# One ones-matmul per head instead of several: VectorE adds key tiles elementwise before TensorE sums over partitions

## What is computed

```python
s = jnp.einsum('bhtd,bhsd->bhts', qb, kb) * jnp.exp(dlog - m_t[..., None])
num = jnp.einsum('bhts,bhsd->bhtd', s, vb) + inter[..., None] * jnp.einsum('bhvk,bhtk->bhtv', C, qb)
den = jnp.sum(s, axis=-1) + inter * jnp.einsum('bhk,bhtk->bht', n, qb)
h = num / jnp.maximum(jnp.abs(den), jnp.exp(-m_t))[..., None]
n_new = decay[..., None] * n + jnp.einsum('bht,bhtk->bhk', wk, kb)
...
hm = hm * lax.rsqrt(jnp.mean(hm * hm, axis=-1, keepdims=True) + EPS)
```

## Time and profile before

| what | value |
|---|---|
| time, median of 3 runs | 1107.98 us (1105.71 to 1108.42) |
| the profiled execution's own time | 1107.28 us |
| its span in the trace | 1105.5 us |
| TensorE busy | 980.7 us, 89% |
| VectorE busy | 675.6 us, 61% |
| ScalarE busy | 551.7 us, 50% |
| GpSimd busy | 286.7 us, 26% |
| mean granted TensorE clock | 0.947 of full |

### The profile page before, as it was taken

How to read it: one execution, slowest core, us unless ns; L and a number is a source line. 1 busy time by engine, 2 the same in 40 slices (tenths; PEclk the granted TensorE clock), 3 DMA queues, 4 the chain that set the end, 5 groups by cost and what they waited for, 6 DMA issues and landing times.

```text
span 1105.5 us, 16710 instructions
## 1 busy us (share of the span) xinstructions
PE 980.7 (89%) x5991; PEld 864.3 (78%) x5991; DVE 675.6 (61%) x820; ACT 551.7 (50%) x610; POOL 286.7 (26%) x192
## 2 busy tenths in 40 slices
PE   3989899999999969799999999837699999999950
PEld 2989789889978958699999976736588888888740
DVE  5495569658848863512111113377889898989738
ACT  5644524715544451423333214434777888887624
POOL 3443213403412240633434433010011110101024
PEclk9989999999999989899999999958899999999985
DMA  9342221313212200123233277135999999999734
GB/s 310 115 158 59 63 67 46 93 38 85 71 48 67 76 19 20 58 77 95 79 92 92 79 197 276 68 128 206 380 397 411 412 414 410 413 413 410 283 113 169
DMA packets 146737, 193.66 MB, mean 175 GB/s; under 512 B 14486, under 2 KB 91692, under 8 KB 146576
## 3 DMA queue, kind: packets, MB, share of 16 engines
q1 hardware_dynamic: 139000, 165.27, 43.4%
q0 software_dynamic: 4656, 16.21, 3.8%
q10 hardware_dynamic: 3048, 11.75, 2.7%
HBM read 173.43 MB, written 19.77 MB: 175 GB/s over the span
## 4 chain that ended last, share of the span: by engine, by line
PE 72%; DVE 14%; issue 5%; DMA 4%; ACT 4%; POOL 0%; DVEq 0%; SPq 0%; ACTq 0%; POOLq 0%
PE PJ L447 58%; DVE MEM L1629 2%; DVE MEM_R L1835 2%; PE MS L1285 2%; PE NM L1265 2%; PE PJ L1214 1%; PE MS L1247 1%; PE MS L1448 1%; DMA CHUNK<-in_w_up_dram 1%; DMA RAW<-in_w_out_dram 1%; PE MS L1292 1%; PE MS L1260 1%; DMA MEM<-t_rows,MEM 1%; PE NM L1479 1%; PE NM L1396 1%
## 5 line engine op out<-in xcount | busy, mean ns | idle before, releaser
L447 PE MATMUL PJ<-MEM_R 128*128 128x272 f32 (+2 forms) x5016 | 812.8, 323 | 22.3 <-DVE MEM_R L1945 6.8
L447 PEld LDWEIGHTS PJ<-MEM_R 128*128 128x128 f32 x5016 | 730.5, 193 | 86.3 <-issue 10.3
L660 POOL TENSOR_TENSOR MEM_R<-RAW,MEM_R 128x1024 fp32r<-128x1024 f32 x81 | 201.5, 2495 | 374.9 <-ACT MEM_R L796 374.7
L1835 DVE TENSOR_TENSOR MEM_R<-CHUNK,MEM_R 128x2048 fp32r<-128x2048 f32 x100 | 224.9, 2287 | 29.1 <-ACT MEM_R L1054 28.9
L1054 ACT CAST MEM_R<-CHUNK 128x2048 fp32r<-128x2048 f32 x100 | 189.5, 1914 | 30.7 <-DMA CHUNK<-in_w_gate_dram 16.0
L796 ACT CAST MEM_R<-RAW 128x1024 fp32r<-128x1024 f32 x81 | 84.6, 1053 | 133.7 <-DMA RAW<-in_w_pb_dram 39.3
L1775 DVE TENSOR_TENSOR MERGED<-PJ,MEM 128x544 f32<-128x544 f32 x16 | 11.6, 724 | 148.4 <-PE PJ L447 148.4
L742 POOL COPY MEM<-MEM 128x1 uint32 (+1 forms) x18 | 17.0, 946 | 268.3 <-PE MS L1448 242.9
L1629 DVE SCALAR_TENSOR_TENSOR MEM<-MEM 128x548 f32<-128x548 f32 x72 | 60.9, 845 | 8.5 <-DVE MEM L1629 0.5
L1063 ACT CAST MEM_R<-MS 128x1024 fp32r<-128x1024 f32 x17 | 17.3, 1016 | 35.3 <-PE MS L1448 35.3
L1247 PE MATMUL MS<-MEM 128*128 128x512 f32 (+4 forms) x80 | 23.3, 437 | 11.7 <-DVE MEM L1669 11.6
(11 more groups left out here) (285 smaller groups left out, 942.5 us busy)
## 6 DMA issues: line engine op xcount, KB each, us to landing
CHUNK<-in_w_gate_dram SPq DMA_DIRECT2D x34, 1024.0 KB, 6.8
CHUNK<-in_w_up_dram SPq DMA_DIRECT2D x34, 1024.0 KB, 8.5
CHUNK<-in_w_down_dram SPq DMA_DIRECT2D x34, 1024.0 KB, 7.0
RAW<-in_w_in_dram SPq DMA_DIRECT2D x56, 512.0 KB, 3.7
expert_rows<-MEM ACTq DMA_DIRECT2D x16, 512.0 KB, 6.0
expert_rows<-MEM SPq DMA_DIRECT2D x8, 512.0 KB, 5.2
RAW<-in_w_pa_dram SPq DMA_DIRECT2D x8, 512.0 KB, 3.7
RAW<-in_w_pb_dram SPq DMA_DIRECT2D x8, 512.0 KB, 3.6
```

What stands on the lines that cost most here:

```text
L447: ins = pe.matmul(out, w(a), x(b), start=first and n == 0, stop=last and n == 2)
L660: tt(lo, raw[slot], hi.bitcast(F32), ALU.subtract).then_inc(lo_done, 1)
L1835: tt(moe_hl[c][1], moe_raw[c], moe_hl[c][0].bitcast(F32), ALU.subtract).then_inc(chunk_lo[c], 1)
```

## The change

In `probabilities`, after the weighted keys, VectorE adds the four key tiles' `dp` for queries 128 to 511 into a new tile `dsum` (three adds of 384, 256 and 128 columns; it lies in the place of `sq`), and the four prompt tiles of `kw` into `ksum` (one add of 512 columns, one of 256; it lies in `rs[:, 1]`). A new step `squares_sum` adds the two channel tiles of `sq` in place (544 columns); it stands between `distances(hd)` and `new_state(hd-1)`, in the last head between `head_results` and `new_state`. TensorE's use 9 is then two matmuls, the first tile's queries 0 to 127 (128 columns) and `dsum` (384 columns), in place of four of 512, 384, 256 and 128; use 13 has one 256-column matmul for the prompt in place of four; uses 14 and 15 have one matmul each in place of two. Three semaphores carry the new waits.

```diff
@@ -195,6 +195,7 @@
         ri = tmp[:, 0:2, :], at("kw", 2, LN_)
         hh = at("tmp", CT, N)
         sq = at("tmp", CT, N, plus=CT * N)
+        dsum = at("tmp", LP - P, plus=CT * N)
         dp = at("dp", J, 512)
         v, kw = at("v", J, HD), at("kw", J, HD)
         c0, c0t = at("c0", CT, HD), at("c0t", CT, HD)
@@ -202,6 +203,7 @@
         nout = at("nout", 2, HD)
         og = at("og", CT, N)
         rs = at("rs", 2, N)
+        ksum = at("rs", 2, HD, plus=N)
         qs = at("qs", CT, LS)
         n0rep = at("n0rep", CT, P)
         n0row = at("n0row", HD)[0:1]
@@ -362,6 +364,7 @@
         conv_done, sig_ready, silu_done = sem("conv_done"), sem("sig_ready"), sem("silu_done")
         decay_ready, poly_ready, root_ready, lru_done = sem("decay_ready"), sem("poly_ready"), sem("root_ready"), sem("lru_done")
         sq_ready, rms_root, my_done = sem("sq_ready"), sem("rms_root"), sem("my_done")
+        dsum_ready, ksum_ready, sq_summed = sem("dsum_ready"), sem("ksum_ready"), sem("sq_summed")
         branch_hi, last_states, rows_copied = sem("branch_hi"), sem("last_states"), sem("rows_copied")
         branch_split = [sem(f"branch_split{m}") for m in range(2)]
         mix_full, sig_done, mul_done, merged_split = sem("mix_full"), sem("sig_done"), sem("mul_done"), sem("merged_split")
@@ -391,7 +394,7 @@
         NCONST, NLATE = 12, 13
         ORDER = [JP] + list(range(JP))
         HALF = D // 2
-        V_HEAD = 61
+        V_HEAD = 64
         FIN_P = 3
         NCT2 = D // P
         NPJ, NMS = PJ_LOOP + (H - 1) * PJ_HEAD, MS_PRE + H * MS_HEAD
@@ -1256,9 +1259,9 @@
             def numerators(hd):
 
                 b = ms_use(9, hd)
-                for j in range(JP):
-                    last = pe.matmul(b[:, P * j:LP], ones, dp[:, j, P * j:LP], start=j == 0, stop=j == JP - 1)
-                filled(last)
+                pe.wait_ge(dsum_ready, hd + 1)
+                pe.matmul(b[:, 0:P], ones, dp[:, 0, 0:P], start=True, stop=True)
+                filled(pe.matmul(b[:, P:LP], ones, dsum, start=True, stop=True))
                 pe.wait_ge(nm_free, hd + 1)
                 for c in range(CT):
                     for j in range(JP):
@@ -1286,19 +1289,15 @@
                                              start=j == tiles[0], stop=j == tiles[-1])
                     filled(last)
                 b = ms_use(13, hd)
-                for m, tiles in enumerate((range(JP), [JP])):
-                    for j in tiles:
-                        n = rows_of[j]
-                        last = pe.matmul(b[:, m * HD:(m + 1) * HD], ones[0:n, :], kw[0:n, j, :], start=j == tiles[0], stop=j == tiles[-1])
-                filled(last)
+                pe.wait_ge(ksum_ready, hd + 1)
+                pe.matmul(b[:, 0:HD], ones, ksum[:, 0, :], start=True, stop=True)
+                filled(pe.matmul(b[:, HD:2 * HD], ones[0:LS, :], kw[0:LS, JP, :], start=True, stop=True))
 
             def head_squares(hd):
-                pe.wait_ge(sq_ready, hd + 1)
+                pe.wait_ge(sq_summed, hd + 1)
                 for u, toks in ((14, slice(0, LP)), (15, slice(LP, N))):
                     b = ms_use(u, hd)
-                    for c in range(CT):
-                        last = pe.matmul(b[:, 0:toks.stop - toks.start], ones, sq[:, c, toks], start=c == 0, stop=c == CT - 1)
-                    filled(last)
+                    filled(pe.matmul(b[:, 0:toks.stop - toks.start], ones, sq[:, 0, toks], start=True, stop=True))
 
             for g in range(4):
                 project(0, g)
@@ -1678,6 +1677,17 @@
                     ins = ts(kw[0:n, j, :], b[0:n, (j % 2) * HD:(j % 2) * HD + HD], gcol[0:n, j, ds(hd + H, 1)], None, ALU.mult)
                     emptied(ins) if j % 2 or j == JP else st.do(ins)
 
+                st.link(tt(dsum, dp[:, 0, P:LP], dp[:, 1, P:LP], ALU.add))
+                st.link(tt(dsum[:, P:], dsum[:, P:], dp[:, 2, 2 * P:LP], ALU.add))
+                tt(dsum[:, 2 * P:], dsum[:, 2 * P:], dp[:, 3, 3 * P:LP], ALU.add).then_inc(dsum_ready, 1)
+                dve.wait_ge(ms_free, hd * MS_HEAD + (MS_PRE + 2 + 9))
+                st.link(tt(ksum, kw[:, 0:2, :], kw[:, 2:4, :], ALU.add))
+                tt(ksum[:, 0, :], ksum[:, 0, :], ksum[:, 1, :], ALU.add).then_inc(ksum_ready, 1)
+
+            def squares_sum(hd):
+                dve.wait_ge(sq_ready, hd + 1)
+                tt(sq[:, 0, :], sq[:, 0, :], sq[:, 1, :], ALU.add).then_inc(sq_summed, 1)
+
             def head_results(hd):
 
                 den, b = misc(hd, 9), misc(hd, 10)
@@ -1741,6 +1751,7 @@
                 head_results(hd - 1)
                 silu(hd, 0)
                 distances(hd)
+                squares_sum(hd - 1)
                 new_state(hd - 1)
                 conv(hd, 1)
                 conv(hd, 2)
@@ -1753,6 +1764,7 @@
                 second_part(hd)
             probabilities(H - 1)
             head_results(H - 1)
+            squares_sum(H - 1)
             new_state(H - 1)
             mean_squares(H - 1)
             branch_rows(H - 1)
```

## The result

| | before | after |
|---|---|---|
| median of its runs | 1107.03 us (1105.71 to 1108.42, 4 runs) | 1094.63 us (1094.31 to 1095.30, 4 runs) |
| profiled execution: span, mean granted clock | 1105.5 us, 0.947 | 1092.1 us, 0.949 |

The ratio of the times, after over before, is 0.9892 with a 95% interval of 0.9875 to 0.9910: the changed kernel is faster by 12.0 us (10 to 13.8). Two further batches of it gave 0.9906 and 0.9875. One later run of the kernel before fell into a slow state (1443 us, at a mean granted clock of 0.649) and is in no ratio and no mean.

What follows compares the result with a forecast made beforehand. TensorE was taken to bound the heads until the weighted-key sums (L1292), then VectorE's chain up to the values. Gains of 2.6, 2.8, 2.6 and 1.3 us summed to 9.3 us, giving 1098.7 us; range 1095.5 to 1106.

Steps and rivals of the forecast that it cites:

- Step 1: Denominator, use 9 on TensorE: 2.16 us become 0.86, 1.30 us saved a head, on the path in all four.
- Step 2: `dsum` and `ksum` adds on VectorE: 3 us a head, swallowed by its 10.41 us wait before L1686; cost 0.
- Step 3: New normaliser, use 13, before L1708: 2.56 us become about 1.0, 1.5 us saved in each of three passes.
- Step 4: Squares, uses 14 and 15: 2.08 us halved to 1.04, but the values' wait grows to some 1.5; gain 0.
- Step 5: `squares_sum` before L1705: 0.73 us add passes GpSimd's L660; L1292 about 0.2 us later in passes one and three, hidden in two.
- Step 6: Last head: L1720's pair waits for GpSimd's L694, which moves by step 1 alone; gain 1.3 us, 3.8 if neither is caught.
- GpSimd gets in first: Rival, chance 0.34: GpSimd's L660 blocks `squares_sum`, delaying L1705 and L1292; gain only 3.9 us, 1104.1 us.
- Everything counts: Rival, chance 0.05: all TensorE savings, squares included, count, 3.84 us in each of four heads, 15.3 us; 1092.7 us.
- The clock falls: Rival, chance 0.07: TensorE idles longer at the values or before L1292, adding 1.2 GHz stretches of 1.4 us each; 1112.5 us.

Runs made afterwards that it cites:

- its own experiment: The kernel before with only the `ksum` part, that is use 13's prompt matmuls and its two adds: ratio 0.9943, 6.3 us faster.
- the old kernel's third trace: The kernel before, unchanged, traced again to compare stages: span 1104.4 us.
- the kernel with the add 0.16 us behind: The changed kernel with a tiny memset and a wait for its end in front of the squares' add: 1101.45 us, ratio 0.9941.

## Why the prediction was right, and by how much it missed

- **Step 1**, right: 0.87 us are left of 2.16, the pass is 1.3 us shorter by it.
- **Step 2**, right: cost 0, with 2.9 us in hand before L1263 and 6.93 us of wait left on VectorE.
- **Step 3**, right in place, 0.2 us too large: the four records take 1.26 us to the next projection and not four tenths of 2.56; 1.31 us saved by its own experiment.
- **Step 4**, right: values wait 1.50 us (1.50 and 1.49 in the other passes), squares alone 0.9995.
- **Step 5**, right in what happened and in its price, where the pass has no slow stretch: the add passed, L1715 came late by a little, and it costs 0.17 us a pass where I had 0.2. The 1.14 us that L1715 waits in the rows of the first pass are made by the slow `project(0, 2)` ahead of it. It also held up GpSimd by 0.6 us, which I had not foreseen. One reading was wrong: I took the slack of 1.73 us before L1705 for a property of the second pass. It belongs to the slow stretch of `project(hd, 2)` and moves with it, so the second pass gains no more than the others. Timeline of VectorE in the old kernel's third trace, whose slow stretch is in pass three, passes two and three:

```profile
246.05 0.69 DVE L1705 COPY MEM<-MS 128x512 f32<-128x512 f32 x1 [0.34 <-PE MS L1285]
...
341.96 0.69 DVE L1705 COPY MEM<-MS 128x512 f32<-128x512 f32 x1 [1.84 <-PE MS L1285]
```

- **The three passes** together: I had 2.6 + 2.8 + 2.6 = 8.0 us, the stretches without slow clock show 3 x 2.44 = 7.3. Step 3's 0.2 us three times is most of the difference.
- **Step 6**, right: L1730 lasts 4.85 us, the pair hangs on L697, and L697 moved by step 1 alone. Step 1 gives 1.28 us, and the pair's end comes 0.2 us nearer to L697's start (13.12 before, 12.91 after): 1.5 us. The other 0.7 of the stage's 2.2 I put down to the clock, by the 5.46 against 4.75 us; no run shows it for the whole stage.
- **The step that failed** is the sentence "What follows (merge, experts) is released by the heads and just moves", with the silent one that the clock's stretches stay as many and as costly as they were; the sum put both at nothing. The edit itself gave 7.3 + 1.5 = 8.8 us, 0.5 less than forecast. The means of the traces differ by 13.3 us. Of the rest, 1.2 us lie in the start and passes one to three ((1.6 + 3.3 + 3.6) less 7.3): half a slow stretch fewer per trace, worth 0.7, and a start that is 0.4 us shorter before the heads' loop. 0.7 us are the last head's, put down to the clock, and 2.6 us lie behind the heads, where the kernels' instructions are the same. The timed runs say that the amount of time at 1.2 GHz is only part of it: it is 117.3 us before and 115.3 after (means of 70 and 16 runs), worth 1.0 us of the 3.5 by which the mean gain of 12.3 exceeds 8.8.

The miss of the range is small: 1094.63 us lies 0.9 us below 1095.5, and the base of the forecast, the median of three runs, itself fell by 0.95 us when a fourth was added (1107.98 to 1107.03). The steps' 9.3 us were near the edit's 8.8; the 3.5 us beyond them stood in no term.

Of the rivals: "GpSimd gets in first" is what the kernel with the add 0.16 us behind does, and at the measured median of 1101.45 us it came out 2.7 us better than the 1104.1 worked out for it, with the clock's part in it larger than its own. "Everything counts" had the end nearest to the measured time, 1092.7 us, and is wrong all the same: the wait for the values grew to 1.5 us. It becomes half true with `conv(hd, 1)` moved. "The clock falls" was not seen at the values: the 1.50 us wait is followed by 14.54 us for 120 records, as before. It was seen behind the 2.26 us wait.

**What stays open.** Whether the new kernel has fewer slow stretches in passes two and three by its nature (six of eight against one of ten speaks for it, the one more in pass one against it) and why, as no run here changed the clock's history alone; and where the 2.6 us behind the heads come from. They are no accident of one trace, as the means over all timed runs differ by 12.3 us too (1107.2 against 1094.9). By half of the slow time behind the heads, which is 2.7 us less on average, 1.3 us of them are the clock's; for the rest no run shows a cause, and nothing was tried that would part the two.

## What to carry to other kernels

Ask at each saved instruction which wait ends last behind it: the same two-for-one edit gave 1.3 us a pass ahead of VectorE's last wait, and nothing behind it until the work that made that wait was moved to where VectorE idles. Two engines that contend can be decided by a tenth of a microsecond (0.04 us behind passed, 0.16 us behind was blocked), so measure the blocked case before you trust a start time. Before you read a slack as a property of a pass, see in a second trace whether it moves with a stretch at the lower clock. And put the scatter into the range before anything else: the old kernel's batches agreed within 0.3 us and gave no warning, the changed kernel's differed by 3.

## What the runs showed of the hardware that I had not expected

- A two-input add on VectorE that starts after GpSimd's instruction still goes first, if it is close enough: 0.01 us (0.71 us long) and 0.04 us (0.70 us long) behind passed, 0.16 us behind took 2.76 us. So it was in every case: 24 adds that started 0.02 to 0.04 us behind passed, three in each of eight traces of four kernels, and the three that started 0.15 to 0.16 us behind were blocked. The one that lets the other by pays 0.6 us: GpSimd's 2.34 us became 2.93 and 2.95. The Trainium skill, SBUF — State Buffer, section "Who interferes with whom", says that the first to issue has the shared ports; by the starts that the trace shows this is right at 0.16 us and not at 0.04.
- A fill of 0.07 us, issued ahead of a waiting add without a chain between them, has the same start in the trace as the add (149.44 us) and delays nothing: the add takes 0.70 us.
- Stretches at 1.2 GHz come and go between executions of one kernel at the same instructions: 48 records of `project(hd, 2)` took 6.3 or 7.6 to 7.8 us. In the passes of the heads' loop one lengthens the pass by 1.4 to 1.5 us.
